# The first projection in quarters of its contraction, and 32 conditioning blocks multiplied by TensorE in the RWKV loop

## The chip, the cores and the metric

One core of one Trainium2 chip. The metric is the device time of one execution in microseconds; the kernel before was run three times.

## What is computed

A trunk of two layers on x of 256 tokens by 2048. Each layer is a token mixer and a SwiGLU FFN, each as

```python
shift, scale, gate = split(silu(c) @ ada_w[i, m] + ada_b[i, m])
h = x * (1.0 + scale) + shift
x = layer_norm(ALPHA * x + (1.0 + gate) * f(h))
```

So four conditioning vectors of 3 x 2048 values come from one vector c and four matrices of 2048 x 6144. In layer 0, f is mixer AB: z = h @ ab_w_in (2048 x 6608), an RWKV-7 mixer of 16 heads in both directions on one part of z's columns, a gated linear attention (GLA) of four heads on the rest, and an output projection. All of it is float32.

## The kernel before, in words

**Numbers and products.** A float32 product is made of three fp32r products: `high` (L473, ScalarE) rounds a loaded block `raw` to `wh`, `low` (L479, VectorE) makes the rest `wl`, and `multiply` (L620, TensorE) issues hi x hi, hi x lo and lo x hi. A unit is one block of 512 columns (the last of 464) by a quarter of the contraction, four tiles of 128 rows: 2 token tiles x 4 x 3 = 24 matmuls. `raw` has four slots, `wh` and `wl` two; unit q is rounded when unit q-2 is multiplied.

**Conditioning by VectorE.** A column of the matrix product is a sum over 2048 rows. VectorE multiplies the loaded tile k of 128 rows by column k of `silu_c` and adds it to an accumulator, so 16 steps leave 128 partial rows per column; TensorE sums these over the partitions with blocks of the accumulator as weights and one column of ones as the moving operand (`cond_cols`, L609, and `part_cols`, L539 with its matmuls at L545: 16 products of 128x128 weights by one column, each issued as two instructions). `cond_unit` (L498) does blocks of 512 columns ahead of the projection, the four of JOBS = (0, 1, 4, 5): the first 1024 columns of shift and scale. `part_step` (L519) does 2048 columns a step with two slots `adaw` for the loads, and is woven into later stages by `cond_step` (L536).

**The first projection.** 13 blocks, 52 units. `block_of` orders them in halves of the contraction: units 0 to 25 take quarters 0 and 1 of every block, units 26 to 51 quarters 2 and 3. A block's two units accumulate in one PSUM bank pair; ScalarE copies the first half's sum to z, and VectorE adds the second half's (`back_sum`, L1827). h is made from x by `turn_pe`, `turn_act` and `turn_dve` (L668, L689, L728): four of its eight groups before unit 0, and two each behind units 19 and 21, once the other half of shift and scale is there. VectorE's program in this stage is `low`, `back_sum`, then one `cond_step`, in all 48: the second half of shift and scale, the gate, and the next shift.

**The RWKV loop.** Turns t = -2 to 8, one pair of heads each, written out by hand in each engine's program. Turn t solves a triangular system for pair t by levels (`level_q` on TensorE, a mask on VectorE, `level_v` on TensorE, a copy to R_V on ScalarE), carries the state of pair t-1 by `chain_x`, `chain_u` and `chain_s`, and prepares pairs t+1 and t+2 (`up_rates`, `head_sums`, `scores`, `z_turn`, `up_decays`, `first`). These products are of 64 x 64 tiles (L2375). VectorE does one `cond_step` a turn, eight in all, for the next scale. The last level's W is accumulated in a bank of its own, L3, which ScalarE seeds (L1489) and copies out (L1494). The GLA is woven into turns 7 and 8 and follows them. Then come the output projection, with eight more `cond_step`, and the FFN.

**Queues.** SyncE issues all loads of weights in order, each behind the semaphore that frees its slot; ScalarE issues small ones.

## Time and profile before

| | us |
|---|---|
| median of three runs | 2799.78 |
| lowest, highest | 2799.08, 2800.55 |
| span of the profiled execution | 2795.5 |
| the median less this span | 4.3 |
| TensorE busy in the span | 2607.3 |
| VectorE busy in the span | 1998.5 |

The profile is of one execution. Its times are us from its first instruction; what lies around the span is the 4.3 us of the table. TensorE's matmuls overlap in the rows, so its busy time says that it had work and not that the array was full. The granted clock is given as a share of full speed: 1.00 is 2.4 GHz, 0.50 is 1.2 GHz, and a value between them is the mean of a stretch.

### The profile page before, as it was taken

The numbers are of one execution on the slowest core, as the hardware profiler recorded it, in microseconds if no ns is written. First come the engines' busy times: TensorE is split into PE (matmuls) and PEld (weight loads), VectorE is DVE, ScalarE is ACT, GpSimd is POOL, SyncE is SP. The second block draws the span as 40 slices with busy tenths as digits, with TensorE's granted clock in tenths as the row PEclk, the third lists the DMA queues.
The fourth block names the chain that finished last, engine by engine and source line by source line (L and its number), as shares of the span: only waits on it lengthen the run. The fifth ranks groups of instructions, "written<-read, shape, count | busy, mean of one in ns | idle before, by whom it ended". The sixth has DMA issues, their size and how long they took to land. (4 is left out here: it accounts for less than half of the span.)

```text
span 2795.5 us, 40258 instructions
## 1 busy us (share of the span) xinstructions
PE 2607.3 (93%) x16814; PEld 2162.9 (77%) x16814; DVE 1998.5 (71%) x1887; ACT 1138.2 (41%) x1295; POOL 272.1 (10%) x199
## 2 busy tenths in 40 slices
PE   1999978888899999999999899999999999999996
PEld 1788858887777888888888678888778888888885
DVE  6778957776686888888888778865668755555557
ACT  1443335555434333333333345545443333333332
POOL 0000000000004000000000086641040000000000
PEclk9999989998999999999999999999999999999998
DMA  9999921110766888888888367754568755555552
GB/s 350 330 335 369 375 70 41 41 38 2 270 233 240 327 304 329 302 328 304 327 305 322 126 211 250 271 166 142 174 237 316 260 195 184 191 194 184 192 193 78
DMA packets 252881, 636.56 MB, mean 228 GB/s; under 512 B 10223, under 2 KB 17061, under 8 KB 230597
## 3 DMA queue, kind: packets, MB, share of 16 engines
q1 hardware_dynamic: 246578, 621.84, 61.9%
q10 hardware_dynamic: 6162, 12.72, 1.2%
q8 instruction: 105, 1.72, 0.3%
q14 instruction: 36, 0.29, 0.0%
HBM read 632.42 MB, written 2.10 MB: 227 GB/s over the span
## 5 line engine op out<-in xcount | busy, mean ns | idle before, releaser
L482 DVE TENSOR_TENSOR s_wl<-s_raw,s_wh 128x2048 fp32r<-128x2048 f32 x393 | 914.4, 2327 | 490.1 <-ACT s_wh L477 481.9
L477 ACT ACTIVATE s_wh<-s_raw 128x2048 fp32r<-128x2048 f32 x396 | 758.4, 1915 | 1163.6 <-PE pa L642 502.6
L640 PE MATMUL pa<-s_wh,s_hth 128*128 128x512 f32 x1616 | 646.2, 400 | 17.2 <-DVE s_wl L482 11.9
L641 PE MATMUL pa<-s_wl,s_hth 128*128 128x512 f32 x1616 | 634.7, 393 | 0.0
L642 PE MATMUL pa<-s_wh,s_htl 128*128 128x512 f32 x1616 | 634.5, 393 | 0.0
L640 PEld LDWEIGHTS pa<-s_wh,s_hth 128*128 128x128 f32 x1616 | 307.3, 190 | 92.0 <-DVE s_wl L482 15.5
L642 PEld LDWEIGHTS pa<-s_wh,s_htl 128*128 128x128 f32 x1616 | 306.8, 190 | 65.6
L529 DVE SCALAR_TENSOR_TENSOR s_wide<-s_adaw,s_silu_c,s_wide 128x2048 f32<-128x2048 f32 x150 | 351.9, 2346 | 5.3 <-DMA s_adaw<-in_ada_w 5.2
L641 PEld LDWEIGHTS pa<-s_wl,s_hth 128*128 128x128 f32 x1616 | 307.5, 190 | 60.3
L640 PE MATMUL pb<-s_wh,s_hth 128*128 128x512 f32 (+1 forms) x816 | 318.8, 391 | 0.0
L642 PE MATMUL pb<-s_wh,s_htl 128*128 128x512 f32 (+1 forms) x816 | 318.6, 390 | 0.0
L641 PE MATMUL pb<-s_wl,s_hth 128*128 128x512 f32 (+1 forms) x816 | 318.4, 390 | 0.0
L640 PE MATMUL py<-s_wh,s_guh 128*128 128x512 f32 x640 | 251.2, 392 | 4.4 <-DVE s_ysum L1071 4.4
L642 PE MATMUL py<-s_wh,s_gul 128*128 128x512 f32 x640 | 249.2, 389 | 0.0
L641 PE MATMUL py<-s_wl,s_guh 128*128 128x512 f32 x640 | 249.1, 389 | 0.0
L640 PEld LDWEIGHTS pb<-s_wh,s_hth 128*128 128x128 f32 x816 | 154.1, 189 | 32.4 <-DVE s_wl L482 0.7
L641 PEld LDWEIGHTS pb<-s_wl,s_hth 128*128 128x128 f32 x816 | 154.0, 189 | 31.8
L642 PEld LDWEIGHTS pb<-s_wh,s_htl 128*128 128x128 f32 x816 | 153.9, 189 | 31.7
L879 POOL TENSOR_TENSOR s_small<-s_small 128x2 f32<-128x2 f32 x4 | 3.8, 946 | 1583.3 <-DVE s_small L868 1583.3
L1071 DVE TENSOR_TENSOR s_ysum<-s_ysum,py 128x512 f32<-128x512 f32 x172 | 116.4, 683 | 47.2 <-PE py L642 46.9
L640 PEld LDWEIGHTS py<-s_wh,s_guh 128*128 128x128 f32 x640 | 120.1, 188 | 35.3 <-DVE s_ysum L1071 7.7
L642 PEld LDWEIGHTS py<-s_wh,s_gul 128*128 128x128 f32 x640 | 120.1, 188 | 25.2
(371 smaller groups left out, 2611.1 us busy)
## 6 DMA issues: line engine op xcount, KB each, us to landing
s_raw<-in_ffn_w_in SPq DMA_DIRECT2D x176, 1024.0 KB, 5.2
s_adaw<-in_ada_w SPq DMA_DIRECT2D x160, 1024.0 KB, 6.2
s_raw<-in_ffn_w_out SPq DMA_DIRECT2D x88, 1024.0 KB, 7.6
s_raw<-in_ab_w_in SPq DMA_DIRECT2D x48, 1024.0 KB, 8.5
s_raw<-in_diff_w_in SPq DMA_DIRECT2D x48, 1024.0 KB, 5.2
s_raw<-in_ada_w SPq DMA_DIRECT2D x16, 1024.0 KB, 8.4
s_raw<-in_ab_w_out SPq DMA_DIRECT2D x16, 1024.0 KB, 10.0
s_qkv<-in_ada_w SPq DMA_DIRECT2D x16, 1024.0 KB, 7.3
```

What stands on the lines that cost most here:

```text
L477: act.activation(wh[:, s % 2, :, 0:width], raw[:, s, :, 0:width], ACT.Copy).then_inc(hi_done, 1)
L482: dve.tensor_tensor(wl[:, s % 2, :, 0:width], raw[:, s, :, 0:width], wh[:, s % 2, :, 0:width].bitcast(F32), ALU.subtract).then_inc(lo_done, 1)
L529: dve.scalar_tensor_tensor(wide[:], frm, silu_c[:, bass.ds(k, 1)], wide[:], ALU.mult, ALU.add).then_inc(ada_step, 1)
L640: pe.matmul(o, a_hi, w_hi, start=start and k == 0, stop=False)
L641: pe.matmul(o, a_hi, w_lo, start=False, stop=False)
L642: mm = pe.matmul(o, a_lo, w_hi, start=False, stop=stop and k == UK - 1)
L879: pool.tensor_tensor(small[:, 38:40], small[:, 34:36], small[:, 95:96].to_broadcast((P, NT)), ALU.pow).then_inc(end_rstd, 1)
L1071: dve.tensor_tensor(y, y, py[:, i], ALU.add).then_inc(py_free, 1)
```

## The change

The conditioning ahead of the first unit shrinks to JOBS = (0, 4), the first 512 columns of shift and scale. The projection runs in four sweeps over the 13 blocks, one quarter of the contraction each, with the block of 464 columns first. Every unit ends its own sum in PSUM; banks pa and pb alternate. ScalarE copies sweep 0 to z, VectorE adds sweeps 1 to 3. Two groups of h are turned ahead of unit 0 and two near the end of each of sweeps 0 to 2. The next quarter of shift and scale comes in eight pairs of half steps a sweep, and sweep 3 does the first half of the gate in the same way. 32 blocks of 2048 x 128 (the second half of the gate, the next shift, half of the next scale) are loaded in the RWKV loop and multiplied by TensorE with the loaded block as weights and a column of `silu_c` as the moving operand, in two halves of eight products, and VectorE adds all of them once in turn 8. Another eight pairs go with the output projection. L3 is given to these sums; the last W is seeded and made in V's bank, L2.

```diff
-        L1, L2, L3 = py[:, 0], pt[:, 0], pa[:, 0]
+        L1, L2, BURST = py[:, 0], pt[:, 0], pa[:, 0]
-        G_gate, G_qk = (P2, P1, P3, P2), (L2, L1, L2, P2)
+        G_gate, G_qk = (P2, P1, P3, P2), (L1, L2, L1, P2)
...
-        JOBS = (0, 1, 4, 5)
+        JOBS = (0, 4)
+        BLOCK_ORDER = (ABC - 1, *range(ABC - 1))
+        FIRST_UNITS = 4 * ABC
+        PAIR_LOADS = 8
+        BURSTS = 32
+        LOAD_AT = [ABC * s + 2 + i for s in range(3) for i in range(PAIR_LOADS)] + [3 * ABC + 1 + i for i in range(PAIR_LOADS)]
+        BURSTS_IN = {-2: 1, -1: 3, 0: 4, 1: 4, 2: 4, 3: 4, 4: 3, 5: 3, 6: 3, 7: 3}
...
+        def burst_load(sp, b):
+            n = BURST_LOADS + b
+            if b < 2:
+                sp.wait_ge(ada_step, JOB_STEPS + 2 * (n - 1))
+            else:
+                sp.wait_ge(burst_done, 2 * (b - 1))
...
+            to = adaw[:, n % 2].rearrange("p (k n) -> p k n", k=KT)
+            src = ada_w.rearrange("a b (k p) n -> (a b) p k n", p=P)[m, :, :, at:at + P]
+            sp.dma_start(to, src).then_inc(wide_in[n % 2], 16)
...
+        def pair_step(dve, n):
+            i = n % PAIR_LOADS
+            dve.wait_ge(*loaded(n))
+            at = JOB_STEPS + 2 * n if n < BURST_LOADS else TAIL_STEPS + 2 * (n - TAIL_LOADS)
+            for kk in range(2):
+                frm, to, k = adaw[:, n % 2, kk * D // 2:(kk + 1) * D // 2], wide[:, 0:D // 2], 2 * i + kk
+                if k == 0:
...
+                else:
+                    dve.wait_ge(ada_step, at + kk)
+                    dve.scalar_tensor_tensor(to, frm, silu_c[:, k:k + 1], to, ALU.mult, ALU.add).then_inc(ada_step, 1)
+        def half_cols(pe, m, steps):
+            pe.wait_ge(ada_step, steps)
+            pe.wait_ge(ada_out, len(JOBS) + m)
+            for j in range(PAIR_LOADS):
+                mm = pe.matmul(pt[:, 1, j:j + 1], wide[:, j * P:(j + 1) * P], ones[:, 0:1], start=(j == 0), stop=True,
+                               skip_group_check=True)
+            mm.then_inc(ada_cols, 1)
+        def burst(pe, b, half):
+            n = BURST_LOADS + b
+            if half == 0:
+                pe.wait_ge(*loaded(n))
+            col = BURST[:, half * BURSTS + b:half * BURSTS + b + 1]
+            block = adaw[:, n % 2].rearrange("p (k n) -> p k n", k=KT)
+            for k in range(half * KT // 2, (half + 1) * KT // 2):
+                mm = pe.matmul(col, block[:, k], silu_c[:, k:k + 1], start=(k == half * KT // 2),
+                               stop=(k == (half + 1) * KT // 2 - 1), skip_group_check=True)
+            mm.then_inc(burst_done, 1)
...
         def block_of(q):
-            half, n = divmod(q, 2 * ABC)
-            return n // 2, 2 * half + n % 2
+            return BLOCK_ORDER[q % ABC], q // ABC
...
+            def summed(q):
+                c = block_of(q)[0]
+                cols = slice(c * W, c * W + width_of(c))
+                dve.wait_ge(in_done, q + 1)
+                dve.wait_ge(z0_out, min(q - ABC + 1, ABC))
+                dve.tensor_tensor(z[:, 0, cols], z[:, 0, cols], (pa, pb)[q % 2][:, 0, 0:width_of(c)],
+                                  ALU.add).then_inc(z0_summed, 1)
...
+            for q in range(FIRST_UNITS):
+                s, m = divmod(q, ABC)
                 low(dve, q // 4, q % 4, width_of(block_of(q)[0]))
+                if q - 2 >= ABC:
+                    summed(q - 2)
+                if s < 3 and m == ABC - 3:
+                    quarter_store(dve, s + 1)
+                    first_factors(dve, s + 1)
+                if s < 3 and m == ABC - 1:
+                    turn_dve(dve, 0, 0, part=s + 1)
+                if q in LOAD_AT:
+                    pair_step(dve, LOAD_AT.index(q))
...
+                for i in range(NT):
+                    if i == 0 and q >= 2:
+                        pe.wait_ge(*((z0_out, q - 1) if q - 2 < ABC else (z0_summed, q - 1 - ABC)))
...
+                if s < 3 and m == ABC - 4:
+                    half_cols(pe, s, JOB_STEPS + 2 * PAIR_LOADS * (s + 1))
+                if s < 3 and m == ABC - 3:
+                    pe.wait_ge(ada_out, len(JOBS) + s + 1)
+                    turn_pe(pe, 0, range(2 * s + 2, 2 * s + 4))
...
             def last_seed(t):
                 act.wait_ge(wt_ready, 4 * t + 4)
-                act.activation(L3, flat(R_W), ACT.Copy).then_inc(ws_ready, 1)
+                act.wait_ge(vc_ready, 5 * t + 5)
+                act.activation(L2, flat(R_W), ACT.Copy).then_inc(ws_ready, 1)
...
                 if n:
-                    pe.wait_ge(vc_ready, 5 * n)
+                    pe.wait_ge(wf_ready, n)
...
+            def bursts(t, at):
+                first_half = 2 * sum(BURSTS_IN[i] for i in range(-2, t))
+                if lev and at < 6:
+                    mine = (at,)
+                elif lev:
+                    mine = range(6, 2 * BURSTS_IN[t])
+                else:
+                    mine = range(2 * BURSTS_IN[t]) if at == 6 else ()
...
                 if lev:
+                    bursts(t, 0)
                     level_q(t, 2)
                 if chain:
                     chain_x(c, 1)
+                if lev:
+                    bursts(t, 1)
...
                 if m < PAIRS:
                     z_turn(m)
                     up_decays(m)
+                if t < PAIRS:
+                    bursts(t, 6)
                 if front:
                     first(n)
```

On TensorE the bursts stand ahead of level_q at levels 2, 3 and 4 and behind chain_x at steps 1, 2 and 3, a half load each; what is left of a turn's loads stands ahead of `first`.

## Rows read from the trace of the kernel before

**Rows 1.** the page's head and its first part, engine busy time

```profile
span 2795.5 us, 40258 instructions
...
PE 2607.3 (93%) x16814; PEld 2162.9 (77%) x16814; DVE 1998.5 (71%) x1887; ACT 1138.2 (41%) x1295; POOL 272.1 (10%) x199
```

**Rows 2.** stages (length; busy PE, PEld, DVE, ACT, POOL; clock, DMA, GB/s)

```profile
41.75:64.17 22.42, 3.73 (x16) 3.56 (x16) 21.93 (x36) 1.03 (x1) 0.00 (x0) 1.00 1.05 387
...
73.28:377.84 304.56, 302.91 (x1360) 252.53 (x1360) 243.57 (x140) 115.55 (x92) 0.00 (x0) 0.98 0.89 333
...
493.79:526.97 33.18, 29.16 (x757) 26.91 (x757) 24.76 (x54) 17.47 (x38) 1.01 (x1) 1.00 0.14 43
...
626.51:692.67 66.16, 53.97 (x1076) 47.45 (x1076) 44.97 (x97) 33.30 (x73) 2.01 (x2) 0.87 0.01 2
```

**Rows 3.** TensorE's waits in four turns, 493.79 to 626.51 (us, times, longest)

```profile
PE pb L2375 <- ACT s_R_U L1504: 8.0, 12, 0.7
PE py L2375 <- ACT s_R_V L1484: 4.6, 8, 0.7
PE pt L2375 <- DVE s_xt L1924: 3.5, 4, 0.9
```

**Rows 4.** timeline of TensorE, products of two conditioning jobs (start, us)

```profile
41.76 1.86 PE L609 MATMUL pt<-s_cst,s_wide 128*128 128x1 f32 x8 [13.97 <-DVE s_wide L517]
...
64.17 1.86 PE L609 MATMUL pt<-s_cst,s_wide 128*128 128x1 f32 x8 [9.20 <-DVE s_wide L517]
```

**Rows 5.** timeline of TensorE, the second part_cols (start, us)

```profile
270.18 3.63 PE L545 MATMUL pt<-s_cst,s_wide 128*128 128x1 f32 x32
```

**Rows 6.** TensorE in the stretches behind the three part_cols; the clock stands behind PE

```profile
173.09:182.69 9.60, 9.60 (x46) 0.64 0.85 303
...
270.18:278.20 8.02, 8.02 (x46) 0.79 0.69 241
...
363.00:370.50 7.50, 7.50 (x42) 0.77 0.02 5
```

**Rows 7.** TensorE by line and form, 73 to 380: turning two groups of h

```profile
L679 PE MATMUL pb<-s_cst,s_xt 128*128 128x128 f32 x8 | 1.2, 273 | 0.0
```

**Rows 8.** TensorE's waits, 73 to 378

```profile
PE pa L640 <- DVE s_wl L482: 3.5, 3, 1.8
```

**Rows 9.** VectorE by line and form, 73 to 380 (busy us, mean ns)

```profile
L482 DVE TENSOR_TENSOR s_wl<-s_raw,s_wh 128x2048 fp32r<-128x2048 f32 x48 | 110.0, 2291 | 30.4 <-ACT s_wh L477 30.4
L529 DVE SCALAR_TENSOR_TENSOR s_wide<-s_adaw,s_silu_c,s_wide 128x2048 f32<-128x2048 f32 x45 | 105.6, 2347 | 5.3 <-DMA s_adaw<-in_ada_w 5.2
...
L1827 DVE TENSOR_TENSOR s_z<-s_z,pb 128x512 f32<-128x512 f32 x12 | 8.2, 681 | 0.0
```

**Rows 10.** VectorE by line and form, whole span: the same operation on 1024

```profile
L2315 DVE SCALAR_TENSOR_TENSOR s_xt<-s_xt,s_small,s_lnb 128x1024 f32<-128x1024 f32 x4 | 5.0, 1281 | 0.1
```

**Rows 11.** timeline of one unit of the projection

```profile
227.32 0.40 PE L640 MATMUL pb<-s_wh,s_hth 128*128 128x512 f32 x1
...
229.22 2.29 DVE L482 TENSOR_TENSOR s_wl<-s_raw,s_wh 128x2048 fp32r<-128x2048 f32 x1 [0.84 <-ACT s_wh L477]
...
231.44 2.35 DVE L529 SCALAR_TENSOR_TENSOR s_wide<-s_adaw,s_silu_c,s_wide 128x2048 f32<-128x2048 f32 x1
...
232.78 0.39 PE L640 MATMUL pb<-s_wh,s_hth 128*128 128x512 f32 x1
```

**Rows 12.** timeline of TensorE in the head of the loop

```profile
391.55 1.22 PE L2407 MATMUL py<-s_raw 96*128 96x256 f32 x2 [0.34 <-ACT s_R_zo L1416]
...
410.51 1.15 PE L2375 MATMUL pt<-s_cst,s_R_W 64*64 64x64 f32 x32 [0.20 <-DVE s_R_W L1944]
```

**Rows 13.** TensorE from 390 to 407.90, the clock behind PE

```profile
390.00:407.90 17.90, 8.65 (x43) 0.50 0.06 16
```

More of the change, by code:

```diff
@@ L539, in part_cols @@
-        def part_cols(pe, g, bank=None):
-            pe.wait_ge(ada_step, g * 16 + (PART_STEPS + 16))
-            pe.wait_ge(ada_out, g + FIRST_JOBS)
-            bank = pt[:, 1] if bank is None else bank
-            for m in range(KT):
-                mm = pe.matmul(bank[:, m:m + 1], wide[:, m * P:(m + 1) * P], ones[:, 0:1], start=(m == 0),
-                               stop=True, skip_group_check=True)
-            mm.then_inc(ada_cols, 1)
         def fold_turn(dve, g):
@@ L2141, in _ @@
                     first(n)
-                if lev and not gla:
-                    cond_step(dve, 32 + t)
                 if gla:
@@ L2338, in _, with first_unit @@
             cond_cols(pe, 0, first=True)
[L2339 to L2340 removed]
+            cond_cols(pe, 1)
             pe.wait_ge(x_in_sem, 16)
[L2342 to L2343 removed]
+            turn_pe(pe, 0, range(0, 2))
+            def first_unit(q):
                 c, s = block_of(q)
[L2345 to L2361 removed]
@@ L2362, in _ @@
-            pe.wait_ge(back_free, 2 * ABC)
+                bank, width = (pa, pb)[q % 2], width_of(c)
+                pe.wait_ge(lo_done, q + 5)
+                if q % ABC == 0:
+                    pe.wait_ge(h_lo, 2 * s + 2)
+                for i in range(NT):
+                    if i == 0 and q >= 2:
+                        pe.wait_ge(*((z0_out, q - 1) if q - 2 < ABC else (z0_summed, q - 1 - ABC)))
+                    elif i == 1 and q >= 2:
+                        pe.wait_ge(*((z1_out, q - 1) if q - 2 < ABC else (z1_summed, q - 1 - ABC)))
+                    for k in range(UK):
+                        a_hi, a_lo = hth[:, UK * s + k, i * P:(i + 1) * P], htl[:, UK * s + k, i * P:(i + 1) * P]
+                        w_hi, w_lo = wh[:, q % 2, k, 0:width], wl[:, q % 2, k, 0:width]
+                        o = bank[:, i, 0:width]
+                        pe.matmul(o, a_hi, w_hi, start=k == 0, stop=False)
+                        pe.matmul(o, a_hi, w_lo, start=False, stop=False)
+                        mm = pe.matmul(o, a_lo, w_hi, start=False, stop=k == UK - 1)
+                    mm.then_inc(unit_done if i else in_done, 1)
@@ new lines, in _ @@
+            for q in range(FIRST_UNITS):
+                s, m = divmod(q, ABC)
+                first_unit(q)
+                if s < 3 and m == ABC - 4:
[3 more added lines that the diff above has]
+                    turn_pe(pe, 0, range(2 * s + 2, 2 * s + 4))
+                if q == FIRST_UNITS - 3:
+                    half_cols(pe, 3, TAIL_STEPS)
+            pe.wait_ge(z0_summed, FIRST_UNITS - ABC)
@@ L2508, in last_w @@
                 for u in range(NU):
-                    mm = two(unit(L3, u), R_Q[:, u], R_W[:, u])
+                    mm = two(unit(L2, u), R_Q[:, u], R_W[:, u])
                 mm.then_inc(w_done, 1)
@@ L2673, in gla_turn_out @@
                 mm.then_inc(g_oT, 1)
+            halves = [(b, half) for b in range(BURSTS) for half in range(2)]
+            def bursts(t, at):
[6 more added lines that the diff above has]
+                    mine = range(2 * BURSTS_IN[t]) if at == 6 else ()
+                for i in mine:
+                    burst(pe, *halves[first_half + i])
             for t in range(-2, PAIRS + 1):
@@ L2794, in _ @@
             out_pe(pe, 13, 13, 0, ready=split_lo, last=lambda: gla_turn_out(GH - 1))
-            part_cols(pe, 2)
+            half_cols(pe, 4, TAIL_STEPS + 2 * PAIR_LOADS)
             pe.sem_inc(pb_free, 2)
```

262 lines of the change are left out of this document (132 added, 130 removed).

## The prediction

> **What bounds the kernel now.** I read the page first, for the span [rows 1], then the view of stages, where the reader is to compare TensorE's busy time with each stage's length [rows 2], and last the timeline and the waits inside the stages that the change touches. Until 64.17 us TensorE has almost nothing to do: VectorE folds four column blocks of conditioning weights, 21.93 us busy of the 22.42 us in which the last two are done. The first projection then takes 304.56 us with TensorE busy for 302.91: it is bound by TensorE. So is the RWKV loop, which is less plain: one turn of it lasts 33.18 us, TensorE works 29.16 of them, VectorE 24.76. The remaining 4.0 us are three waits for a chain's U, two for V and one for a product of VectorE [rows 3]. TensorE runs its program in order, so an instruction added there costs its length, except where it stands just ahead of one of those waits.
>
> **The start.** The jobs go from four to two. The second ended with its column products at 41.76 us, the fourth at 64.17 [rows 4]; the chain from the last job to the first product at 73.28 is the same, as unit 0 needs only the first quarter of h. The DMA queue delivers in the same order, weights in the place of the third job. Minus 22.4 us.
>
> **The projection, TensorE.** 52 units of the same 24 matmuls stay. Three calls of part_cols at 3.63 us (32 instructions, 0.113 us each) [rows 5] become four of half the size inside the projection: 4 x 1.81 - 3 x 3.63 = -3.6. Each part_cols also brought the granted clock down: the mean was 0.64 over 9.60 us, 0.79 over 8.02 and 0.77 over 7.50 [rows 6], that is 3.5 + 1.7 + 1.7 = 6.9 us lost, though TensorE was busy without a pause. I take it that 1.81 us do not bring it down (between -6.9 and +2.3 for the four). A third turning of h: its matmuls 1.2 us [rows 7], its wait like that of the two before, which with the start's 1.8 make up the 3.5 us of waits in this stretch, 0.85 each [rows 8]: +2.0.
>
> **The projection, VectorE.** In every unit it makes w_lo (2.29 us); in three quarters of them it now adds two partial sums (0.68 each), and in 8 units of every sweep it takes two loads of half width [rows 9]. A step of 2048 lasts 2.35; the same operation on 1024 lasts 1.28 elsewhere [rows 10]. The second step of a pair waits for the first. Two instructions in a row overlap by 0.07 (229.22 + 2.29 against 231.44). So 2.29 + 1.36 + 2.56 - 4 x 0.07 = 5.93, some 6.0 with the wait inside a pair. A unit of TensorE takes 5.46 (from 227.32 to 232.78, 24 matmuls) [rows 11]. The excess is 0.54, and the slack is small: rounding by ScalarE starts when a unit ends, and high, low and the first sum fill nearly the whole next unit. 8 x 0.54 less 0.1 is 4.2 us a sweep, in three sweeps: +12.7 (6 if the excess is a quarter us, 18 if the sums are hit by more waits). Sweep 0 has no sums: 2.29 + 2.56 fits, as does ScalarE with its copies. What goes, 48 steps of 2.35 us, was hidden. DMA carries 84 loads in place of 100 in a stretch that had room (333 GB/s) [rows 2], and a pair has two units' time to land: nothing. quarter_store waits on VectorE for half_cols, with low behind it; it comes in units without a pair step, so nothing is late. Sum: -3.6 - 6.9 + 2.0 + 12.7 = +4.2. **First projection and start together: -18.2.**
>
> **The RWKV loop.** Each of 32 loads is now multiplied by TensorE: 16 matmuls of 128x128 weights by one column, 32 instructions. part_cols is exactly this form, so a load costs 3.63 us at full clock and a half 1.81. At the lower level (0.50, 1.2 GHz) the eight instructions of a job took 1.86 [rows 4], so 7.4 a load. VectorE loses eight steps of 2.35 us; at 24.76 of 33.18 it did not bind. Turn by turn:
> - Turn -2, one load, placed behind up_decays and ahead of the products at 391.55, for which all of this head waits. The clock was 0.50 there, and the wait 0.34 [rows 12, 13]: +7.1. ScalarE's sigmoid, the square, the norm and VectorE's factors queue behind it.
> - Turn -1, three loads just ahead of the first product of the chain at 410.51, which had waited 0.20. After a part_cols began, the clock stood for 2.7, 4.6 and 4.1 us (what is left of each stretch of [rows 6] when its mean is split into 1.00 and 0.50); 4 us at full and the other 61 instructions at 0.23 make 18.2, and some 1.7 us are lost until dense work raises it again: +19.7. The wait for the fourth block's DMA hides in it.
> - Turns 0 to 3, four loads each: 14.5 less the 0.87 of the wait for VectorE [rows 3], which has more time now. The U waits stand between chain_u and chain_s and the V waits behind first and level_v; no burst is put there, so they stay. 4 x 13.6 = +54.5. The last two halves stand together, as long as a part_cols: 2.3 us of lowered clock each, +9.2.
> - Turns 4 to 6, three loads: 3 x (10.9 - 0.9) = +30.
> - Turn 7, three loads, where TensorE was busy 53.97 of 66.16 us [rows 2] and waited for VectorE, which loses a step: I take 5 of the 10.9 us as hidden, +5.9.
>
> **The last W in V's bank** makes ScalarE's seed follow its own copy of V and the next first() follow the copy of W; three and more us of score and output products lie between on TensorE. Nothing, and at most 0.6 us a turn if that cover is gone. The GLA head takes other banks and one more wait: nothing. The output projection's eight steps become eight pairs, 8 x 0.2 us more on VectorE beside TensorE, and half a part_cols goes: nothing.
>
> **Sum:** -18.2 + 7.1 + 19.7 + 54.5 + 9.2 + 30 + 5.9 = +108 us. 2795.5 becomes 2903.7. The median of the runs, 2799.78, stands 4.3 above this span, so 2908.
>
> **A rule against a row.** TensorE did not pause in the 9.60 us over which the clock fell [rows 6]; matmuls of one column were enough. The Trainium skill (TensorE: Matmul & The Clock Gate, "Why this matters for your kernels") ties the loss of throughput in mid-kernel to gaps in which TensorE is idle. By that rule the bursts in turns -1 to 3 would keep the clock, and the sum would be some 18 us lower, 2890. The trace does not agree, so the sum goes by the row.
>
> **The rivals.**
> 1. *The clock goes down again and again in the loop.* Bursts are 1.81 us, but a level holds two of them and a wait in some 9.4 us, and the loop's own products are small. For it: part_cols alone brought it down, three times of three. Against it: in the loop as it is, with 12% of waits, the clock stayed at 1.00. If it is down in 30% of turns 0 to 6, some 290 us of work grow by about 50: 2958.
> 2. *Waits take in more of it.* Later V and U are ready when TensorE comes, and all 4.0 us a turn go, with no fall of the clock: 101.6 - 32 in turns 0 to 7, 7 + 11 ahead of them: 88 - 31 (no overload in the projection either) gives 2857. Against it: the places of the bursts.
> 3. *Faster.* The weight loads of a burst hide behind the products around it, so the loop is free and only the start counts: 2782. It decides from the point at which a burst adds less than 0.6 us a load. Against it: in part_cols each weight load took its 0.113 us with another right behind it, and a matmul of one column covers nothing.
> 4. *The loads on TensorE are not what costs, VectorE is:* if both sums of a unit (1.36 us) stand in the path with some 0.3 us of slack, each of 39 units loses about 1 us, +40 in the place of +12.7, and the loop goes as forecast: 2935. Against it: only the first sum holds back the next unit but one's first tile.
>
> **How the numbers follow.** The forecast 0.62, rival 1 0.18, rival 2 0.12, rival 3 0.03, rival 4 0.05. The range is 2858 to 2966: rival 2 bounds it below, rival 1 above. Differences under 0.2% (5.6 us) can't be told from none here. Slower 0.96, same 0.01, faster 0.03.
>
> **What would show it.** The first unit starts near 51 us. The pair units of sweeps 1 to 3 are 0.5 us longer than others, with TensorE waiting for VectorE's w_lo or sum. The rows of the burst line show 1024 instructions with a busy time of about 116 us or more. A turn with four loads lasts 47 to 50 us, one with three 43; the wait for the xt product is gone and those for U are there. The clock is at 0.50 in the three bursts ahead of the chain. I am wrong if a turn stays under 40 us (the load costs less than part_cols), or if the clock is low through the loop.

## The result and the profile after

The changed kernel takes 2935.85 us (median of 4 runs, 2929.05 to 2944.18) against 2799.43 (2798.28 to 2800.55) for the kernel before, run beside it on the same chip: ratio 1.0493, 95% interval 1.0473 to 1.0513. It is slower by 136 us. The forecast was 2908 us, so the side and the range were right and the number was 28 us too low.

The page of the changed kernel, head, first part, and two of the lines of its second part (40 equal slices of the span: the clock in tenths, and what the DMA engines moved):

```profile
span 2935.3 us, 42283 instructions
...
PE 2770.2 (94%) x17774; PEld 2316.9 (79%) x17774; DVE 1964.4 (67%) x1924; ACT 1138.2 (39%) x1295; POOL 272.0 (9%) x199
...
PEclk9999968979889999999999989999999999999998
...
GB/s 315 295 282 296 204 94 84 89 77 74 49 94 339 179 321 304 329 309 327 311 324 315 298 116 244 234 246 152 187 160 330 284 190 185 197 186 189 195 188 86
```

TensorE is busy 163 us more than in [rows 1], the span is 139.8 us longer, and in the first half of the clock's line the lowered slices (6, 7, 9, 11 and 12) lie between 367 and 881 us, which is the RWKV loop and its surroundings.

The stages of the changed kernel (length; busy PE, PEld, DVE, ACT, POOL; clock, DMA, GB/s). The first row is the last conditioning job, the second the start of the first product, the third the projection, the fourth the head of the loop:

```profile
18.00:40.30 22.30, 1.87 (x8) 1.78 (x8) 17.52 (x29) 0.00 (x0) 0.00 (x0) 1.00 1.04 396
40.30:50.30 10.00, 3.68 (x17) 3.28 (x17) 6.01 (x10) 6.33 (x8) 0.00 (x0) 1.00 1.05 386
50.30:355.20 304.90, 298.60 (x1336) 243.36 (x1336) 245.49 (x210) 116.46 (x94) 0.00 (x0) 1.00 0.80 278
355.20:385.20 30.00, 14.88 (x58) 12.54 (x58) 10.68 (x24) 12.02 (x23) 2.17 (x4) 0.59 0.21 54
```

Against [rows 2] the projection starts 23.0 us earlier and is as long as before (304.9 against 304.56), now at clock 1.00 in place of 0.98. So the kernel is 22.6 us ahead when the projection ends (355.20 against 377.84), and everything that it loses, it loses behind that.

The loop, from the first bonus product of TensorE (a mark that stands once in every turn) to the first transpose of the GLA outputs, first in the kernel before, then in the changed one:

```profile
408.09:708.80 300.71, 259.25 (x6133) 233.91 (x6132) 216.92 (x461) 157.99 (x347) 10.10 (x10) 0.97 0.10 30
```

```profile
391.42:849.30 457.88, 428.99 (x7126) 397.40 (x7125) 202.82 (x455) 158.29 (x348) 10.10 (x10) 0.85 0.27 73
```

The loop grew by 157 us, and the mean granted clock in it went from 0.97 to 0.85. The marks of the changed kernel show where:

```profile
606.96 0.48 PE L2660 MATMUL pb<-s_R_rkr,s_cst 128*128 128x256 f32 x1
...
669.96 0.48 PE L2660 MATMUL pb<-s_R_rkr,s_cst 128*128 128x256 f32 x1
...
714.11 0.48 PE L2660 MATMUL pb<-s_R_rkr,s_cst 128*128 128x256 f32 x1
...
758.26 0.48 PE L2660 MATMUL pb<-s_R_rkr,s_cst 128*128 128x256 f32 x1
```

The mark stands ahead of a turn's last halves, so the seven stretches between two marks hold six loads (the three of turn -1 among them), four times four, and twice three. They last 61.9, 51.4, 53.1, 49.1, 63.0, 44.15 and 44.15 us, where those of before last 25.1 and then 33.2. Two of them, one with three loads at full clock, one with four at a lower one:

```profile
714.11:758.26 44.15, 41.01 (x856) 38.20 (x852) 22.86 (x52) 17.39 (x38) 1.01 (x1) 1.00 0.28 76
606.96:669.96 63.00, 60.44 (x887) 56.90 (x884) 22.90 (x52) 17.49 (x38) 1.01 (x1) 0.70 0.27 73
```

Inside the slow one (length; busy PE; clock, DMA, GB/s), and with it the row of the late products themselves (busy us, mean ns; they overlap in the rows):

```profile
630.00:640.00 10.00, 9.56 (x103) 0.50 0.40 107
640.00:650.00 10.00, 9.56 (x127) 0.50 0.34 94
```

```profile
L630 PE MATMUL pa<-s_silu_c,s_adaw 128*128 128x1 f32 x1024 | 144.3, 272 | 0.0
```

The 1024 instructions of the 32 loads are busy for 144.3 us, where 32 times the 3.63 us of [rows 5] are 116.2. The clock stood at 0.50 for 20 us in which TensorE was busy for 19.1. That is the extreme; from 420 to 758 us the mean is 0.88, which is the lower level for some 24% of the time:

```profile
420.00:758.26 338.26, 319.38 (x5706) 0.88 0.31 85
```

The waits of the loop are there as forecast, TensorE from 391.9 to 700:

```profile
PE pb L2468 <- ACT s_R_U L1583: 9.1, 15, 0.7
PE py L2468 <- ACT s_R_V L1562: 6.5, 11, 0.7
PE pb L2468 <- issue: 0.3, 1, 0.3
```

Those for U and V stay, 0.6 us each, and the one for VectorE's product [rows 3] is gone.

### The profile page after: what moved, and what is told of

Read it like the earlier page. It is cut to its first block and busy times, and to the rows that moved or that the text cites. A ratio compares the mean times of both kernels' runs of the same rounds, so it can differ in the third digit from the quotient of the medians.

```text
span 2935.3 us, 42283 instructions
## 1 busy us (share of the span) xinstructions
PE 2770.2 (94%) x17774; PEld 2316.9 (79%) x17774; DVE 1964.4 (67%) x1924; ACT 1138.2 (39%) x1295; POOL 272.0 (9%) x199
## 5 line engine op out<-in xcount | busy, mean ns | idle before, releaser
L531 DVE TENSOR_TENSOR s_wl<-s_raw,s_wh 128x2048 fp32r<-128x2048 f32 (+1 forms) x393 | 914.0, 2326 | 500.8 <-ACT s_wh L526 492.2
L724 PE MATMUL pa<-s_wh,s_hth 128*128 128x512 f32 x1312 | 526.4, 401 | 13.9 <-DVE s_wl L531 8.2
L726 PE MATMUL pa<-s_wh,s_htl 128*128 128x512 f32 x1312 | 515.4, 393 | 0.0
L725 PE MATMUL pa<-s_wl,s_hth 128*128 128x512 f32 x1312 | 515.4, 393 | 0.0
L724 PEld LDWEIGHTS pa<-s_wh,s_hth 128*128 128x128 f32 x1312 | 249.0, 190 | 75.8 <-DVE s_wl L531 13.0
L724 PE MATMUL pb<-s_wh,s_hth 128*128 128x512 f32 x704 | 274.4, 390 | 0.0
L725 PE MATMUL pb<-s_wl,s_hth 128*128 128x512 f32 x704 | 274.2, 389 | 0.0
L726 PE MATMUL pb<-s_wh,s_htl 128*128 128x512 f32 x704 | 274.1, 389 | 0.0
L578 DVE SCALAR_TENSOR_TENSOR s_wide<-s_adaw,s_silu_c,s_wide 128x2048 f32<-128x2048 f32 x90 | 211.1, 2345 | 0.0
L630 PEld LDWEIGHTS pa<-s_silu_c,s_adaw 128*128 128x128 f32 x1024 | 141.0, 221 | 6.0 <-issue 2.9
```

What stands on the lines that cost most here:

```text
L531: dve.tensor_tensor(wl[:, s % 2, :, 0:width], raw[:, s, :, 0:width], wh[:, s % 2, :, 0:width].bitcast(F32), ALU.subtract).then_inc(lo_done, 1)
L578: dve.scalar_tensor_tensor(wide[:], frm, silu_c[:, bass.ds(k, 1)], wide[:], ALU.mult, ALU.add).then_inc(ada_step, 1)
L630: mm = pe.matmul(col, block[:, k], silu_c[:, k:k + 1], start=(k == half * KT // 2), stop=(k == (half + 1) * KT // 2 - 1), skip_group_check ...
L724: pe.matmul(o, a_hi, w_hi, start=start and k == 0, stop=False)
L725: pe.matmul(o, a_hi, w_lo, start=False, stop=False)
L726: mm = pe.matmul(o, a_lo, w_hi, start=False, stop=stop and k == UK - 1)
```

## The experiments

Each ratio is to runs of the kernel before on the same chip (2796.7 to 2798.2 us median in the four groups of runs). Differences between two versions are mostly taken from their profiled spans, one execution each.

**1. All but the late products (e5).** This kernel keeps every part of the change except the 512 products of the 32 loads and most of what they load, and so measures the two halves of the sum apart. The columns of the modulation that they carry are not what they should be: the store adds two stretches of `tab` in one instruction, where it had added the products to one of them in two. So they do not hold the table alone, as the expectation has it.

```diff
-            sp.dma_start(to, src).then_inc(wide_in[n % 2], 16)
+            sp.dma_start(to[:, 0:1], src[:, 0:1]).then_inc(wide_in[n % 2], 16)
...
-            for k in range(half * KT // 2, (half + 1) * KT // 2):
-                mm = pe.matmul(col, block[:, k], silu_c[:, k:k + 1], start=(k == half * KT // 2),
-                               stop=(k == (half + 1) * KT // 2 - 1), skip_group_check=True)
-            mm.then_inc(burst_done, 1)
+            pe.sem_inc(burst_done, 1)
```

> The changed kernel without the 512 late products; each of the 32 loads brings one of its 16 rows of blocks and is only counted. Left out: the part of the modulation that these loads carry (its columns hold the table alone). Theory: all that the quarter sweeps, the two jobs less, the other bank and the late output steps do is the start, -23, and a projection of the same length, so the loop goes back to turns of 33.2 us and the time is 2777 us (2770 to 2785). Rival: the bank, the waits for the loads or the late output steps cost something of their own: 2787 or more, with turns above 33.6 us.

Measured: 2778.23 us (2776.80 to 2778.69), ratio 0.9925 (0.9909 to 0.9942). The theory holds. The first row is a turn, the second the whole loop:

```profile
543.59:576.77 33.18, 29.16 (x760) 26.91 (x756) 22.57 (x52) 17.46 (x38) 1.01 (x1) 1.00 0.06 18
...
385.02:688.40 303.38, 261.84 (x6134) 235.79 (x6133) 200.63 (x454) 157.99 (x347) 10.10 (x10) 0.96 0.06 15
```

The turn is back at 33.18 us with the same 29.16 us of TensorE as in [rows 2]. The span is 2776.9: the quarter sweeps and all else that the change does are worth -18.6 us against 2795.5, and the late products cost 2935.3 - 2776.9 = 158.4 us. By the two ratios (1.0493 and 0.9925) it is 159 us, good to some 7 by their intervals.

**2. One product of eight (e1).**

```diff
-            for k in range(half * KT // 2, (half + 1) * KT // 2):
-                mm = pe.matmul(col, block[:, k], silu_c[:, k:k + 1], start=(k == half * KT // 2),
-                               stop=(k == (half + 1) * KT // 2 - 1), skip_group_check=True)
-            mm.then_inc(burst_done, 1)
+            k = half * KT // 2
+            pe.matmul(col, block[:, k], silu_c[:, k:k + 1], start=True, stop=True,
+                      skip_group_check=True).then_inc(burst_done, 1)
```

> The changed kernel, with one of the eight products of each half load left out of nothing but kept, and the other seven left out: 64 products (128 instructions) in the loop in place of 512. All loads, waits, stores and the whole projection stay. Theory (what costs is TensorE's time for the 512 products, 3.6 to 3.7 us a load at full clock, and the clock that they bring down): 64 x 0.227 = 14.5 us stay, the start still gives 23 back, the clock in the loop is as before: 2793 us (2786 to 2802). Rival (the loads in rows of 512 bytes, their waits, or the other edits of the loop cost a part of it): 2830 or more.

Measured: 2807.27 us (2803.90 to 2809.49), ratio 1.0029 (1.0016 to 1.0041), span 2806.7, above the 2793 that I expected and below the rival's 2830. Its span less that of e5 is 29.8 us, and the trace has two parts for it. One is a wait for a load, which the full products had covered:

```profile
395.88 1.01 PE L630 MATMUL pa<-s_silu_c,s_adaw 128*128 128x1 f32 x4 [5.51 <-DMA s_adaw<-in_ada_w]
```

The other part is that each of the 64 half loads costs (29.8 - 5.5) / 64 = 0.38 us on average, though one product is two instructions of 0.113 us, 0.23. So 0.15 us a half go beside the instructions themselves, 9.6 us in all; a turn with three loads in six places shows it too:

```profile
568.94:604.41 35.47, 31.84 (x772) 1.00 0.37 99
```

(35.47 - 33.18) / 6 = 0.38. The average is rough: in the head of the loop and in turns 0 to 3 some halves stand together, and the clock was low in a part of the head. What makes the 0.15 us, wherever a burst breaks into the row of small products, stays open.

**3. A moving operand of 64 columns (e4).** The instructions are the same in number, weights and order; only the moving operand is silu's column 64 times over. The sums fall on one another in the bank, so those 32 blocks of the modulation are not what they should be.

```diff
-            col = BURST[:, half * BURSTS + b:half * BURSTS + b + 1]
+            at = 64 * (2 * b % 8 + half)
+            col = BURST[:, at:at + 64]
...
-                mm = pe.matmul(col, block[:, k], silu_c[:, k:k + 1], start=(k == half * KT // 2),
+                mm = pe.matmul(col, block[:, k], silu_c[:, k:k + 1].to_broadcast((P, 64)), start=(k == half * KT // 2),
```

> The changed kernel with 64 equal columns in place of one as the moving operand of each product of a load; the output leaves out what these loads should give, as their sums overwrite one another. Theory (the weight load sets the 0.113 us of an instruction, and one-column products bring the granted clock down): an instruction stays at 0.113 to 0.12, the clock in the loop stays at 1.00, and the 40 us or so that the low clock costs come back: 2893 (2885 to 2910). Rival 1 (64 columns make an instruction longer, by half or more): 2980 and up. Rival 2 (the clock falls for another reason than the few columns): 2936 within 8.

Measured: 2898.65 us (2896.19 to 2900.83), ratio 1.036 (1.0343 to 1.0378), 37 us less than the changed kernel though each product does 64 times the work. A turn of four loads, the loop, and the row of the late products:

```profile
539.11:587.09 47.98, 44.84 (x886) 41.91 (x884) 22.92 (x52) 17.52 (x38) 1.01 (x1) 1.00 0.35 96
...
388.47:807.30 418.83, 386.29 (x7125) 355.52 (x7124) 202.67 (x455) 158.29 (x347) 10.12 (x10) 0.96 0.29 79
```

```profile
L631 PE MATMUL pa<-s_silu_c,s_adaw 128*128 128x64 f32 x1024 | 130.9, 285 | 2.4 <-DMA s_adaw<-in_ada_w 2.4
```

The mean clock in the loop is 0.96, as it is in e5 with no late product at all, and the four stretches of four loads all last 48.0 us. A load still takes 3.68 us, against 3.63 for one column. So the clock is a cause by itself: with only the number of moving columns changed it stays up from turn 0 to turn 6, and 2935.3 - 2896.8 = 38.5 us come back (37 by the ratios, good to some 7). In the head it was not held: between the first two marks of e4 the mean is 0.86, and TensorE waits 2.4 us for a load there.

**4. Eight columns (e4b).** Each sum has eight columns of its own and the output is whole.

```diff
-            col = BURST[:, half * BURSTS + b:half * BURSTS + b + 1]
+            at = 8 * (half * BURSTS + b)
+            col = BURST[:, at:at + 8]
...
-                mm = pe.matmul(col, block[:, k], silu_c[:, k:k + 1], start=(k == half * KT // 2),
+                mm = pe.matmul(col, block[:, k], silu_c[:, k:k + 1].to_broadcast((P, 8)), start=(k == half * KT // 2),
...
-            dve.tensor_tensor(to, to, BURST[:, BURSTS:2 * BURSTS], ALU.add).then_inc(burst_out, 1)
+            dve.tensor_tensor(to, to, BURST[:, 8 * BURSTS:16 * BURSTS:8], ALU.add).then_inc(burst_out, 1)
```

> The late products with a moving operand of 8 equal columns in place of 1, each sum in 8 columns of its own, everything else as in the changed kernel. 64 columns held the granted clock in most of the loop and gave 2899 us. If 8 columns also hold it: 2899 us (2892 to 2906), the turns of four loads near 48 us. If 8 are no better than one: 2936 us (2929 to 2943), turns from 49 to 63 us as before. A value between the two says that the clock is held in a part of the turns only.

Measured: 2927.33 us (2925.38 to 2937.98), ratio 1.0471 (1.0447 to 1.0495).

```profile
389.74:835.00 445.26, 414.48 (x7125) 383.07 (x7124) 202.61 (x455) 158.23 (x347) 10.11 (x10) 0.88 0.27 74
```

A value between the two: the clock in the loop is 0.88, against 0.85 with one column and 0.96 with 64. By the medians eight columns give back 8.5 of the 37 us, but the interval of this ratio and that of the changed kernel overlap, so it is not shown that eight columns are better than one.

**5. No load in the head, four in each turn (e2).**

```diff
-        BURSTS_IN = {-2: 1, -1: 3, 0: 4, 1: 4, 2: 4, 3: 4, 4: 3, 5: 3, 6: 3, 7: 3}
+        BURSTS_IN = {-2: 0, -1: 0, 0: 4, 1: 4, 2: 4, 3: 4, 4: 4, 5: 4, 6: 4, 7: 4}
```

> The changed kernel with no load in turns -2 and -1 and four in each of turns 0 to 7. In the head the first took 6.8 us and the next three 16.4, at the lower clock. Theory (the head was dear because the clock was down and because all waits for it there): four loads at 3.7 us and some falls of the clock in place of 23.2 us and the slow products behind them: 11 us less than the changed kernel, 2925 (2912 to 2934). Rival (four loads cost the same wherever they stand, since four in a turn bring the clock down each time): 2936 within 5.

Measured: 2946.93 us (2944.15 to 2953.44), ratio 1.0538 (1.052 to 1.0555). A miss: I expected the head's low clock to be what the four loads there pay twice for, and a gain of some 10 us. The kernel got 11 us slower.

```profile
385.86:856.00 470.14, 443.33 (x7158) 411.42 (x7157) 203.09 (x455) 158.40 (x348) 10.10 (x10) 0.82 0.26 73
```

The loop's clock is 0.82 in place of 0.85. The six stretches between marks with four loads last 51.4, 51.9, 60.3, 50.3, 58.8 and 50.3 us, so the clock now falls in the later turns too, where three loads had twice lasted 44.15. Taking the loads from the head only moved the falls.

**6. The halves where TensorE waits anyway (e3).** The six halves of a turn stand ahead of level_q(1), behind chain_u(0) to chain_u(3) and behind level_q(5), so that U and V come up meanwhile.

```diff
                 if lev:
+                    bursts(t, 0)
                     level_q(t, 1)
...
                     chain_u(c, 0)
+                if lev:
+                    bursts(t, 1)
...
                 if lev:
-                    bursts(t, 0)
                     level_q(t, 2)
                 if chain:
                     chain_x(c, 1)
-                if lev:
-                    bursts(t, 1)
```

> The changed kernel with the same halves in other places of a turn: ahead of level_q at level 1, behind chain_u at steps 0, 1, 2 and 3 and behind level_q at level 5, where TensorE waited 0.7, 0.65 three times and 0.46 us. Theory (TensorE's program is the bound and only these waits can hide a product): some 3 us a turn, 20 us in all: 2914 (2905 to 2925), and the waits for U and V are gone from the profile. Rival (ScalarE and VectorE become late elsewhere as soon as TensorE no longer waits there): 2930 to 2940.

Measured: 2922.66 us (2919.53 to 2925.28), ratio 1.0443 (1.0425 to 1.046). All that is left of TensorE's waits from 391.9 to 700, and the loop:

```profile
PE pt L2468 <- DVE s_R_Q L2032: 0.5, 2, 0.3
PE pa L630 <- DMA s_adaw<-in_ada_w: 0.4, 1, 0.4
```

```profile
392.65:834.60 441.95, 431.95 (x7125) 405.96 (x7124) 201.33 (x455) 158.92 (x347) 10.11 (x10) 0.83 0.27 75
```

The 15.6 us of waits for U and V are gone, TensorE pauses for 10 us in 442 (29 in 458 before this edit), and the kernel is 13 us faster. But the clock is no higher, 0.83, with TensorE busy for 98% of the stretch.

**7. Both, eight columns in the waits (e7).**

```diff
+                if lev:
+                    bursts(t, 0)
                     level_q(t, 1)
...
+            at = 8 * (half * BURSTS + b)
+            col = BURST[:, at:at + 8]
```

> The 8 equal columns together with the places ahead of the U and V waits. The places alone took 13 us off. If 8 columns hold the clock, the gains add but for what the places saved by way of the clock: 2886 us (2878 to 2893), turns of four loads near 45.5 us (33.2 + 14.5 - 3 of waits). If 8 columns do not hold it: 2922 us (2917 to 2928).

Measured: 2912.89 us (2905.07 to 2921.07), ratio 1.0399 (1.0368 to 1.043), the fastest of the versions that keep the late products on TensorE and the output whole. The result agrees with gains that add up (13.2 and 8.5 are 21.7; 23.0 measured) but cannot show it, with runs 16 us apart, and eight columns did not hold the clock, which is 0.84 in the loop, and the 2886 that I hoped for was missed.

**8. One step of each pair left out (e9).** In sweeps 1 to 3 VectorE skips the second half step of each pair, 24 times 1.28 us; half of what those loads carry is missing from the modulation.

```diff
                     dve.wait_ge(ada_step, at + kk)
+                    if kk and PAIR_LOADS <= n < BURST_LOADS:
+                        dve.sem_inc(ada_step, 1)
+                        continue
```

> In the sweeps 1 to 3 of the first projection the second step of each pair is left out on VectorE (24 steps of 1.28 us; left out: half of the conditioning weights that these pairs carry). If VectorE's total work in the units with a pair is what makes them 5.9 us long, all 24 return to 5.44 us: 2925 us (2922 to 2929), and the waits for w_lo are gone. Rival: the waits come from the order in which the partial sums stand ahead of w_lo, not from the load: 2932 us or more.

Measured: 2931.40 us (2925.71 to 2935.64), ratio 1.047 (1.045 to 1.049). The whole time can't tell, since the changed kernel's runs alone spread over 15 us (their mean clock goes from 0.964 in the fastest to 0.959 in the slowest); the projection's own rows can:

```profile
50.30:348.10 297.80, 294.87 (x1336) 245.71 (x1336) 216.66 (x187) 116.45 (x94) 0.00 (x0) 1.00 0.81 285
```

Its waits from 52 to 348, and those of the changed kernel from 52 to 356:

```profile
PE pa L2443 <- DVE s_z L1908: 1.3, 1, 1.3
PE pb L2443 <- DVE s_z L1908: 1.3, 1, 1.3
```

```profile
PE pa L2440 <- DVE s_z L1905: 3.0, 9, 1.3
PE pb L2440 <- DVE s_z L1905: 3.0, 9, 1.3
```

The projection is 7.1 us shorter (297.8 against 304.9), and of 18 waits for the partial sums 16 are gone. Its first unit happens to last 1.3 us longer than in the changed kernel (7.74 against 6.47); from the start of the second unit to that of the last it is 278.55 us against 287.23, so the second steps cost 8.7. The order of the sums was left alone, so it is the amount of VectorE's work in those units that delayed them.

**9. The bank alone (e6), and wider columns in the kernel before (e8).** The first puts only the last W into V's bank, with the waits and the banks of the GLA head that go with it; the second gives each column product of part_cols 32 equal columns.

```diff
-                act.activation(L3, flat(R_W), ACT.Copy).then_inc(ws_ready, 1)
+                act.wait_ge(vc_ready, 5 * t + 5)
+                act.activation(L2, flat(R_W), ACT.Copy).then_inc(ws_ready, 1)
...
-                    pe.wait_ge(vc_ready, 5 * n)
+                    pe.wait_ge(wf_ready, n)
```

> The kernel before with only the part of the change that puts the last W in V's bank, with its two waits and the banks of the GLA head. Forecast: no change, 2799 us (2796 to 2802). Rival: the wait of ScalarE for its own copies, or of the next first() for the copy of W, shows in every turn: turns of 33.5 us or more in place of 33.18, 2801 to 2805.

```diff
-                mm = pe.matmul(bank[:, m:m + 1], wide[:, m * P:(m + 1) * P], ones[:, 0:1], start=(m == 0),
+                mm = pe.matmul(bank[:, 32 * m:32 * m + 32], wide[:, m * P:(m + 1) * P], ones[:, 0:32], start=(m == 0),
...
-            dve.tensor_tensor(ada_flat[:, bass.ds(g * 16 + 32, 16)], bank[:, 0:16],
+            dve.tensor_tensor(ada_flat[:, bass.ds(g * 16 + 32, 16)], bank[:, 0:512:32],
```

> The kernel before, with one edit: the column products of part_cols take 32 equal columns in place of one (16 times 32 columns fill the bank; part_store reads each 32nd). All instructions stay. Theory: the products of one column bring the granted clock down in the first projection, and wider ones hold it: the 6.9 us lost behind the three calls come back, less what the fourth call does in the output projection: 2792 us (2790 to 2795), the clock at 1.00 behind each call. Rival: something else lowers the clock there: 2799 (2796 to 2802).

Measured: e6 2798.05 us (2795.86 to 2801.27), ratio 1.0003 (0.9994 to 1.0012): no change, as forecast. e8 2798.45 us (2794.59 to 2799.75), ratio 0.9999 (0.999 to 1.0008): a miss. The 6.9 us did not come back, and the rows say why; the first stretch stands behind the first part_cols, the second is that call's own row:

```profile
174.90:184.50 9.60, 9.60 (x46) 8.37 (x45) 5.20 (x5) 2.40 (x2) 0.00 (x0) 0.66 0.89 339
```

```profile
174.89 4.13 PE L545 MATMUL pt<-s_cst,s_wide 128*128 128x32 f32 x32
```

The clock fell all the same, to a mean of 0.66 where it was 0.64 [rows 6]; behind the second call it stayed at 1.00 and behind the third it fell again. So e4 does not carry over: 64 columns kept the clock up in the loop, 32 columns did not keep it up here in two calls of three.

**10. The late loads on VectorE (e10, e11).** Here TensorE gives the late loads back. The same weights come in another cut, 1024 columns of two tiles of rows a load in place of 128 columns of all sixteen. VectorE adds them up in 64 half steps of 1024, put where it waits for TensorE, and TensorE only does four times 8 column products. The outputs are whole.

```diff
+        def late(dve, count):
+            for _ in range(count):
+                b, kk = divmod(next(late_halves), 2)
...
+                dve.scalar_tensor_tensor(to, frm, silu_c[:, k:k + 1], to, ALU.mult, ALU.add).then_inc(late_step, 1)
...
                     mix(n)
+                if lev:
+                    late(dve, 1)
...
                     keys(n)
+                if lev:
+                    late(dve, 1)
...
                     first(n)
+                if lev:
+                    late(dve, 2)
...
                     moments(c)
+                if lev and not gla:
+                    late(dve, 2)
```

> The changed kernel, but the 32 late loads are added on VectorE in 64 half steps (1.28 us each) put into its idle places: 18 between the end of the projection and the end of turn -1, six in each of turns 0 to 6, four in turn 7; TensorE only does four times 8 column products. All outputs are computed. Without the late products the time is 2778 us. VectorE idles some 10 us of a turn of 33 and gets 7.7. Theory: what TensorE pays 158 us for, VectorE does nearly free: 2778 + 4 for the products + 6 of clock + 8 of lateness = 2796 us (2786 to 2812), turns of 33.2 to 35. Rival: the half steps stand in front of work that TensorE waits for, 2 us or more in each turn: 2815 or more.

Measured: 2796.41 us (2794.95 to 2800.63), ratio 0.9995 (0.9986 to 1.0004), where 2796 was expected. A turn with six half steps, TensorE's waits in it, and the half steps' own row:

```profile
486.91:520.09 33.18, 29.16 (x760) 26.91 (x756) 29.53 (x58) 17.46 (x38) 2.01 (x1) 1.00 0.33 106
```

```profile
PE pb L2508 <- ACT s_R_U L1603: 2.0, 3, 0.7
PE py L2508 <- ACT s_R_V L1582: 1.2, 2, 0.7
PE pt L2508 <- DVE s_xt L2031: 0.9, 1, 0.9
```

```profile
L544 DVE SCALAR_TENSOR_TENSOR s_wide<-s_adaw,s_silu_c,s_wide 128x1024 f32<-128x1024 f32 x59 | 75.6, 1282 | 6.7 <-DMA s_adaw<-in_ada_w 2.9 <-issue 0.4
```

The turn is 33.18 us to the hundredth, as in [rows 2], with VectorE busy for 29.53 of it in place of 24.76, and the waits of [rows 3] at a quarter of their sums over four turns, so unchanged. The span is 2795.5, so the 32 loads cost 18.6 us above e5 in this form and 158.4 on TensorE. By the marks those 18.6 us stand in the head (+3.6), behind the first two marks (+1.7, and +4.7 where the first column products are), in the two later turns with column products (+1.7 each), and from the last mark to the GLA outputs (+4.6).

The last run spreads the half steps otherwise and moves the column products into the waits:

```diff
-                    late(dve, 1)
+                    late(dve, 2 if 0 < t < 7 else 1)
...
                     chain_u(c, 1)
+                if t in (1, 3, 5):
+                    burst(pe, t // 2)
```

> The kernel with the late loads on VectorE once more, spread otherwise: 14 half steps up to the end of turn -1 (18 before), six in turn 0, seven in each of turns 1 to 6, two in turn 7; the four groups of 8 column products stand behind chain_u in turns 1, 3, 5 and 7, where TensorE waits for U anyway, in place of the ends of turns 0, 3, 5 and 7 (which were 4.2 and three times 1.7 us longer than a turn of 33.2). All outputs are computed. Theory: the column products at the ends of the turns were most of what was left: 2796 - 6 for them - 2 in the head - 1 behind turn 7 = 2787 us (2782 to 2792), turns of 33.2 to 33.8. Rival: seven half steps are more than VectorE's idle places take, and the turns get longer by the seventh: 2794 or more.

Measured: 2799.22 us (2795.53 to 2807.74), ratio 1.0011 (1.0002 to 1.002). The rival was right: the seventh half step is not free.

```profile
483.38:518.04 34.66, 31.19 (x776) 28.88 (x773) 30.51 (x60) 17.47 (x38) 1.48 (x1) 1.00 0.31 102
```

This turn has column products in it. The turns 1 to 6 last 34.5 to 35.8 us in place of 33.18, those without column products too (34.9 to 35.8), and in two of these (447.61 to 483.38 and 518.04 to 552.96) TensorE waits for a mask of VectorE, for which it does not wait in the turn of e10 shown above:

```profile
PE pt L2507 <- DVE s_R_Q L2055: 0.9, 1, 0.9
...
PE pt L2507 <- DVE s_R_Q L2055: 0.5, 1, 0.5
```

The seventh half step stands right behind another one, ahead of that mask; whether it is the number or this place that costs was not told apart. No version that I ran and that computes the whole output beats the kernel before by more than a measurement can tell; the changed kernel without its late products shows that up to 20 us would be there for one that finds them a place for nothing.

## Why the prediction was right, and where it was short

With e5, e1 and e4 the 139.8 us between the two profiled spans split into five terms:

| term | forecast, us | measured, us | from |
|---|---|---|---|
| start, projection and all else but the late products | -18.2 | -18.6 | e5 |
| 32 loads at full clock | +116.2 | +116.2 | 32 x 3.63 |
| breaking into the loop, 64 half loads | 0 | +9.6 | e1, 64 x 0.15 |
| waits that the bursts take in | -11.3 | -7.5 | e4, below |
| clock lowered by the bursts | +21.5 | +40.1 | the rest |
| sum | +108.2 | +139.8 | |

In e4 the clock was held outside the head, and its loads cost 2896.8 - 2776.9 = 119.9 us; 32 x 3.68 + 9.6 is 127.4, so 7.5 us were hidden (what the clock and a wait for a load still cost in e4's head is inside this, so the last two terms are each good to some 5 us). What then lacks from 158.4 to 116.2 + 9.6 - 7.5 is the clock's 40.1 (38.5 by the difference of the spans of the changed kernel and e4, whose products are 0.05 us a load longer). The forecast's 21.5 are its 3.5 in turn -2, 8.8 in turn -1 and 9.2 in turns 0 to 3; its 11.3 are 0.9 in each of turns 0 to 6 and 5 in turn 7. So the forecast had the price of the loads and the side right, put the break-in at nothing without a reason, and had about half of the clock's cost; its range held because rival 1 had set its upper end at 2966. The measured number is nearer to rival 1's 2958 than to 2908.

- **The start**: -23.0 measured, -22.4 forecast. Right. That the first row of the table agrees to 0.4 us is luck all the same: start and projection together gave -22.6 where -18.2 was forecast, and in e5 the loop (303.38 against 300.71) and what follows it are 2.7 and 1.8 us longer than before.
- **The projection**: +0.3 measured, +4.2 forecast. The clock's 6.9 us came back as taken (1.00 throughout). A pair unit lasts 5.92 us (the next first product at 307.67 behind one at 301.75), just the 5.93 of the working:

```profile
301.75 0.47 PE L2440 MATMUL pb<-s_wh,s_hth 128*128 128x512 f32 x1 [0.20 <-DVE s_z L1905]
...
307.67 0.47 PE L2440 MATMUL pa<-s_wh,s_hth 128*128 128x512 f32 x1 [0.22 <-DVE s_z L1905]
```

  VectorE's overload was mis-sized at 12.7, as 24 units were taken to be that long: the 18 waits say that it held back some 18 of them, and e9 puts it at 8.7 (7.1 by the whole stage). With 8.7 in its place the terms -3.6 - 6.9 + 2.0 + 8.7 make +0.2. Rival 4 (+40 from the sums) gave 2935, nearly the measured number, and only by coincidence: this run and the projection's +0.3 exclude it.
- **Turn -2 and turn -1**: 6.83 and 16.43 us for their loads, where 7.1 and 18.2 were taken, near enough. The price of a load at the lower level (7.4) had been read from [rows 4], but the clock column shows 1.00 in that stage [rows 2], so that row does not show it; the row at 368.33 does, as its clock is 0.50:

```profile
368.33 6.83 PE L630 MATMUL pa<-s_silu_c,s_adaw 128*128 128x1 f32 x32
...
393.48 16.43 PE L630 MATMUL pa<-s_silu_c,s_adaw 128*128 128x1 f32 x96
```

- **Turns 4 to 6**: where the clock stayed up, a turn of three loads lasts 44.15 us, +10.97, against the +10.0 of the forecast. The wait for VectorE went (0.87) and 6 x 0.15 us came.
- **Turns 0 to 3, the step that failed**: "The last two halves stand together, as long as a part_cols: 2.3 us of lowered clock each". The forecast let the clock fall once a turn, behind that pair of halves, and let single halves of 1.81 us pass. Behind each of the four pairs it did fall. But it fell behind single halves too, as in the turn of 606.96 to 669.96, where it was at 1.00 until the single half of 627.00 was through, and then at 0.50 for 20 us on end (630 to 650, above):

```profile
620.00:630.00 10.00, 9.28 (x171) 1.00 0.10 30
...
627.00 1.95 PE L630 MATMUL pa<-s_silu_c,s_adaw 128*128 128x1 f32 x16
```

  Stretches of 49 to 63 us stand in the place of 47 to 50: the four of them are 24.7 us longer than those of e4, where 9.2 were forecast. Rival 1 had this mechanism, with somewhat too large a size (down in 30% of turns 0 to 6, +50 us; the rows say some 24%, and the clock's whole cost is 18.6 us above the forecast's).
- **Rival 2** (the bursts take in all waits and the clock does not fall: 2857) failed in both: the waits for U and V stayed, and the clock fell. Even with the halves put at those waits (e3) the time is 2923.
- **Turn 7**: +14.1 us measured from the last mark to the first transpose of the GLA outputs, +5.9 forecast. In e4 the same stretch is 6.4 us longer than before (807.3 - 724.0 against 708.8 - 631.9). So the 5 us taken as hidden were about right (in e5 the same stretch is 1.6 us longer than before even without the loads), and the other 7.7 us are the clock: its mean in this stretch is 0.79, against 0.90 in e4 and 0.87 before.
- **The V bank, the output steps, the other banks**: nothing that a measurement can tell, as forecast (e6; e5).
- **Rival 3** (bursts free behind other products) would have put TensorE's part at nothing. The turns at full clock, 10.97 us longer for three loads, exclude it.

The rule that was weighed ahead of the result says that throughput in mid-kernel drops with gaps in which TensorE is idle (the Trainium skill, TensorE: Matmul & The Clock Gate, "Why this matters for your kernels"). By that rule the sum would have been 2890, and the trace again does not agree: from 630 to 650 us the clock was 0.50 with TensorE busy for 19.12 of 20 us, and e3, which took nearly every pause out of the loop, does not have the higher clock of the two (0.83 against 0.85, one profile each). In e4 only the number of moving columns was other, and there the clock stayed at 1.00 in the turns of four loads.

## What to carry to other kernels

Before work moves to another engine, compare what it costs there with the idle time of the engine that it leaves: 32 loads cost 158 us on a TensorE that bounds the loop, and 19 us on a VectorE with 10.6 idle us in a turn of 33.18; that idle time took six half steps a turn for nothing, and a seventh, put right behind another, made the turns 1.3 to 2.6 us longer. A matmul of one column costs as much as one of 64 (32 instructions take 3.63 and 3.68 us), so its price is not in its columns, and it can be paid again in the clock of all that stands around it: where the nearest rows show a fall behind one burst, put a fall behind shorter ones into the range too, and not only behind those as long as the one that was seen.

## What the runs showed of the hardware

- The granted clock stood at 0.50 (1.2 GHz) for 20 us on end while TensorE was busy for 96% of them, with the loop's own small products and with bursts of one column. With 64 columns in the late products it was 0.96 over the loop, with 8 columns 0.88 (0.84 with the halves in the waits), with one 0.85 (0.83 there), in one profile each. In another place, behind the first projection's units, 32 columns did not keep it up (0.66 over 9.60 us). What tells these apart stays open.
- The runs of the kernel whose clock falls most spread widest: the changed kernel over 15 us (2929 to 2944), those of e4, with the clock up in the turns, over 4.6, those of the kernel before over 2.3, with four runs each. In eleven and more runs the kernel before and e6 spread over 8.2 and 5.4 us too, so four runs say little of a spread.
- VectorE's multiply-and-add of 1024 took 1282 ns in the loop of e10, while loads arrived at 106 GB/s beside it, and 1281 in [rows 10].
